# A hybrid decoder step: product-key routing over 80 sums instead of 256, 24 expert items in another stage, and FoX heads half a head later

## What is computed

```python
qry = (xi @ w_query).reshape(PEER_BLOCK, PEER_HEADS, 2, PEER_HALF)
s = jnp.einsum('thpc,pnc->thpn', qry, sub_keys)          # 2 x 128 scores per head
s1, i1 = lax.top_k(s[:, :, 0], 16)
s2, i2 = lax.top_k(s[:, :, 1], 16)
cand = (s1[..., :, None] + s2[..., None, :])             # 16 x 16 sums
cidx = (i1[..., :, None] * 128 + i2[..., None, :])
top_s, pos = lax.top_k(cand.reshape(..., 256), 16)
idx = jnp.take_along_axis(cidx, pos, axis=-1)
gate = jax.nn.softmax(top_s, axis=-1)
hid = gelu(einsum('td,thkd->thk', xi, expert_u[idx]))
y = einsum('thk,thkd->td', gate * hid, expert_v[idx])    # 8 heads x 16 experts per token
```

## Time and profile before

| | us |
|---|---|
| runs shown: median of 3 (lowest to highest) | 4675.52 (4673.76 to 4675.54) |
| profiled execution, its own time | 4657.51 |
| its span | 4655.7 |
| busy: PE, PEld, DVE | 2418.1, 1909.2, 3374.0 |
| busy: ACT, POOL | 545.6, 2361.1 |
| moved by DMA | 1513.69 MB, 325 GB/s over the span |

### The profile page before, as it was taken

The page is one execution under the profiler, slowest core; times in us unless marked ns, Lnnn a source line. Parts: engine busy times, 40 slices in busy tenths (PEclk is TensorE's granted clock), DMA queues, the critical chain, the costliest instruction groups (busy, mean ns, idle before and its releaser), DMA issues. The chain is left out here.

```text
span 4655.7 us, 35143 instructions
## 1 busy us (share of the span) xinstructions
PE 2418.1 (52%) x11713; PEld 1909.2 (41%) x11713; DVE 3374.0 (72%) x4421; ACT 545.6 (12%) x1307; POOL 2361.1 (51%) x1217
## 2 busy tenths in 40 slices
PE   6999999898488888888759564200000000000000
PEld 5888888677466656666547443100000000000000
DVE  1333333307749989989877588799898989989998
ACT  1222222200122212222210010000000000000000
POOL 1110001000226676656565322288888888888886
PEclk8999999799699999999859777655555555555555
DMA  6666666386759999999999855499999999999998
GB/s 188 210 189 203 210 203 192 112 291 228 265 209 402 410 391 393 395 391 395 339 363 408 309 203 203 154 416 422 404 419 405 411 413 420 420 412 422 411 417 355
DMA packets 443932, 1513.69 MB, mean 325 GB/s; under 512 B 42044, under 2 KB 276208, under 8 KB 277848
## 3 DMA queue, kind: packets, MB, share of 16 engines
q0 software_dynamic: 161840, 1158.85, 61.7%
q1 hardware_dynamic: 269240, 251.94, 17.0%
q10 hardware_dynamic: 12672, 100.67, 5.4%
HBM read 1384.96 MB, written 126.21 MB: 325 GB/s over the span
## 5 line engine op out<-in xcount | busy, mean ns | idle before, releaser
L1929 DVE SCALAR_TENSOR_TENSOR ex_y<-ex_ring,ex_wt,ex_y 128x2048 f32<-128x2048 f32 x538 | 1264.4, 2350 | 122.5 <-DMA ex_ring<-in_peer_v_dram,idx_all 74.4
L1914 DVE CUSTOM_DVE_ANT_0 ex_ring<-ex_ring,ex_xi 128x2048 f32<-128x2048 f32 x544 | 1244.7, 2290 | 141.2 <-DMA ex_ring<-in_peer_u_dram,idx_all 50.5
L1836 POOL DMA_INDIRECT ex_ring<-in_peer_u_dram,idx_all x384 | 794.4, 2069 | 341.2 <-DVE ex_hid L1914 136.3
L1836 POOL DMA_INDIRECT ex_ring<-in_peer_v_dram,idx_all x384 | 823.5, 2145 | 221.7 <-DVE ex_hid L1914 115.9
L1868 PE MATMUL ex_fold<-ex_y,const 128*32 128x512 f32 (+1 forms) x48 | 24.9, 683 | 1113.4 <-DVE ex_y L1929 1043.5
L1836 POOL DMA_INDIRECT ex_ring<-in_peer_v_dram,ex_idx_s x160 | 316.3, 1977 | 316.2 <-DVE ex_hid L1914 144.6
L1868 PEld LDWEIGHTS ex_fold<-ex_y,const 128*32 128x32 f32 (+1 forms) x48 | 6.3, 136 | 1131.6 <-DVE ex_y L1929 1044.4
L1836 POOL DMA_INDIRECT ex_ring<-in_peer_u_dram,ex_idx_s x160 | 315.1, 1969 | 200.3 <-DVE ex_y L1929 139.7
L843 PE MATMUL heads_b_pj<-xnT_b,lead 128*128 128x304 f32 x1376 | 410.3, 436 | 5.1 <-PEq L270 3.7
L843 PE MATMUL heads_a_pj<-xnT_a,heads_a_w 128*128 128x256 f32 x1216 | 310.1, 393 | 1.7 <-DMA heads_a_w<-in_w_in_dram 1.7
L843 PEld LDWEIGHTS heads_b_pj<-xnT_b,lead 128*128 128x128 f32 x1376 | 255.6, 198 | 79.4 <-issue 15.0
(11 more groups left out here) (568 smaller groups left out, 4156.3 us busy)
## 6 DMA issues: line engine op xcount, KB each, us to landing
lead<-w_scratch SPq DMA_DIRECT2D x43, 1024.0 KB, 9.1
heads_a_w<-in_w_in_dram SPq DMA_DIRECT2D x38, 1024.0 KB, 6.1
w_scratch<-heads_a_w ACTq DMA_DIRECT2D x38, 1024.0 KB, 4.4
lead<-in_w_in_dram SPq DMA_DIRECT2D x26, 1024.0 KB, 5.7
w_scratch<-lead ACTq DMA_DIRECT2D x26, 1024.0 KB, 4.6
heads_b_w<-w_scratch SPq DMA_DIRECT2D x21, 1024.0 KB, 9.5
out_a_w<-in_w_out_dram SPq DMA_DIRECT2D x7, 2048.0 KB, 14.3
w_out_scratch<-out_a_w ACTq DMA_DIRECT2D x7, 2048.0 KB, 9.5
```

The source lines that it names most:

```text
L1836: pool.indirect_dma_start(self.ring[:, i % RING, :], None, self.tables[which], bass.IndirectOffsetOnAxis(ap=self.index(s, g, k), axis=0)). ...
L1914: nc.vector.tensor_tensor_reduce(ring, ring, self.tokens(s)[:], 1.0, 0.0, ALU.mult, ALU.add, self.hid[:, g % 2, k:k + 1]).then_inc(self.se ...
L1929: nc.vector.scalar_tensor_tensor(y, ring, wt, y, ALU.mult, ALU.add).then_inc(self.sem["consumed"], 1)
```

## The change

Three things are changed.

1. **Routing.** With both lists sorted, a pair (i, j) of the 256 can be among the best 16 only if (i+1)(j+1) is at most 16. The 80 sums kept are first[0] with all 16 of second, first[1..7] with second[0..7], and first[8..15] with second[0]. The positions in these 80 are turned back into a pair by five small instructions on VectorE (`last`, `second`, `place`). ScalarE makes the tables of indices (three copies, once `scores_read` is there), minus the best sum (`neg`), and the exponentials with it as bias, one per tile, each with its sum; VectorE's cast of the indices, subtraction, sum over the gates and copy of the index are gone.
2. **Items.** `OVERLAP` gives heads_b 306 items instead of 330 and route_b 72 instead of 48; the total of 448 stays.
3. **Half a head later.** FoX head h begins at mark 100 h + 50. The projections have marks that are 37.5 later, and the gate of GDN (`G_Z`) is projected before FoX's three segments. Items now stand over marks 0 to 850.

```diff
-OVERLAP = {"norm": 14, "heads": 330, "out": 48, "ffn": 8, "route": 48}
+OVERLAP = {"norm": 14, "heads": 306, "out": 48, "ffn": 8, "route": 72}
...
-G_Q, G_K, G_V, F_Q, F_K, F_V, G_Z, F_OG = range(8)
+G_Q, G_K, G_V, G_Z, F_Q, F_K, F_V, F_OG = range(8)
...
 def segment_mark(j, step):
-    return 12.5 * (j - 6) + 12.5 * step / KT
+    return 12.5 * (j - 3) + 12.5 * step / KT
+
+def fox_mark(h):
+    return 100.0 * h + 50
...
             def fox():
                 for h in range(HEADS):
-                    at, n, qkv = 100.0 * h, h + 1, B.f_qkvT[:, h % 2]
+                    at, n, qkv = fox_mark(h), h + 1, B.f_qkvT[:, h % 2]
...
             def items():
                 for i in range(quota):
-                    yield 100.0 * HEADS * (i + 0.5) / quota
+                    yield (100.0 * HEADS + 50) * (i + 0.5) / quota
                     share.take(dve, i + 1)
...
-                act.wait_ge(sem["centred"], h + 1)
-                nc.scalar.activation(B.gate[:], B.gate[:], ACT.Exp).then_inc(sem["exped"], 1)
+                act.wait_ge(sem["scores_read"], h + 1)
+                if h >= 1:
+                    act.wait_ge(sem["picked"], h)
+                nc.scalar.copy(B.table[:, 0, :, 0:1], B.at[:, :, 0, 0:1])
+                nc.scalar.copy(B.table[:, 0, :, 1:], B.at[:, :, 0, :])
+                nc.scalar.copy(B.table[:, 1, :, 0:TOPK], B.at[:, :, 1, :]).then_inc(sem["tabled"], 1)
+                act.wait_ge(sem["best_found"], h + 1)
+                nc.scalar.mul(B.neg[:], B.best[:, :, 0], -1.0).then_inc(sem["negated"], 1)
+                act.wait_ge(sem["negated"], h + 1)
+                for t in range(T):
+                    last = nc.scalar.activation(B.gate[:, t, :], B.best[:, t, :], ACT.Exp, bias=B.neg[:, t:t + 1],
+                                                accum_out=B.sum[:, t:t + 1])
+                last.then_inc(sem["exped"], 1)
...
-                order.mark(nc.vector.tensor_copy(B.atf[:], B.at[:]))
-                order.link(nc.vector.tensor_tensor(B.cand[:], B.top[:, :, 0, :].unsqueeze(3).to_broadcast([P, T, TOPK, TOPK]),
-                                                   B.top[:, :, 1, :].unsqueeze(2).to_broadcast([P, T, TOPK, TOPK]), ALU.add))
-                top16(order, [(B.cand[rows[t], t].rearrange("p a b -> p (a b)"), B.best[rows[t], t, :], B.pos[rows[t], t, :])
-                              for t in range(T)])
-
-                nc.vector.tensor_tensor(B.gate[:], B.best[:], B.best[:, :, 0:1].to_broadcast([P, T, TOPK]), ALU.subtract
-                                        ).then_inc(sem["centred"], 1)
+                first, second = B.top[:, :, 0, :], B.top[:, :, 1, :]
+                order.mark(nc.vector.tensor_tensor(B.cand[:, :, 0:TOPK], first[:, :, 0:1].to_broadcast([P, T, TOPK]), second, ALU.add))
+                order.mark(nc.vector.tensor_tensor(
+                    B.cand[:, :, TOPK:72].rearrange("p t (a b) -> p t a b", b=8),
+                    first[:, :, 1:8].unsqueeze(3).to_broadcast([P, T, 7, 8]),
+                    second[:, :, 0:8].unsqueeze(2).to_broadcast([P, T, 7, 8]), ALU.add))
+                order.mark(nc.vector.tensor_tensor(B.cand[:, :, 72:CANDS], first[:, :, 8:], second[:, :, 0:1].to_broadcast([P, T, 8]),
+                                                   ALU.add))
+                order.wait()
+                if h >= 1:
+                    dve.wait_ge(sem["exped"], h)
+                top16(order, [(B.cand[rows[t], t, :], B.best[rows[t], t, :], B.pos[rows[t], t, :]) for t in range(T)])
+                dve.sem_inc(sem["best_found"], 1)
                 share.take(dve, h * PARTS + 3)
...
                 order.link(nc.vector.tensor_copy(B.posf[:], B.pos2[:]))
+                order.mark(nc.vector.scalar_tensor_tensor(B.last[:], row, 9.0, column, ALU.is_equal, ALU.mult))
+                order.mark(nc.vector.tensor_scalar(B.second[:], row, 1.0, 8.0, ALU.is_equal, ALU.mult))
+                order.wait()
+                order.mark(nc.vector.tensor_tensor(B.place[:, 0], row, B.last[:], ALU.add))
+                order.mark(nc.vector.tensor_tensor(B.place[:, 1], column, B.last[:], ALU.subtract))
+                order.wait()
+                order.link(nc.vector.tensor_tensor(B.place[:, 1], B.place[:, 1], B.second[:], ALU.add))
+                dve.wait_ge(sem["tabled"], h + 1)
...
-                order.link(nc.vector.scalar_tensor_tensor(B.pick[:, 0], B.pick[:, 0], float(KEYS), B.pick[:, 1],
-                                                          ALU.mult, ALU.add))
-                order.mark(nc.vector.tensor_copy(mem["idx_all"][:, group.own, h, :], B.pick[:, 0]))
+                dve.sem_inc(sem["picked"], 1)
+                order.mark(nc.vector.scalar_tensor_tensor(mem["idx_all"][:, group.own, h, :], B.pick[:, 0], float(KEYS),
+                                                          B.pick[:, 1], ALU.mult, ALU.add))
                 dve.wait_ge(sem["exped"], h + 1)
-                order.link(nc.vector.tensor_reduce(B.sum[:], B.gate[:], AX_X, ALU.add))
```

More of the change, by code:

```diff
@@ L47 @@
 KEYS = 128
+CANDS = 80
 SEGS = 4
@@ L2282, in _ @@
+                order.mark(nc.vector.tensor_tensor(B.cand[:, :, 72:CANDS], first[:, :, 8:], second[:, :, 0:1].to_broadcast([P, T, 8]),
[5 more added lines that the diff above has]
+                dve.sem_inc(sem["best_found"], 1)
                 share.take(dve, h * PARTS + 3)
-                order.mark(nc.vector.tensor_scalar(B.pos2[:, 0], B.pos[:], 4, None, ALU.logical_shift_right))
@@ L2285, in _ @@
-                order.mark(nc.vector.tensor_scalar(B.pos2[:, 1], B.pos[:], TOPK - 1, None, ALU.bitwise_and))
+                row, column = B.posf[:, 0], B.posf[:, 1]
+                order.mark(nc.vector.tensor_scalar(B.pos2[:, 0], B.pos[:], 3, None, ALU.logical_shift_right))
+                order.mark(nc.vector.tensor_scalar(B.pos2[:, 1], B.pos[:], 7, None, ALU.bitwise_and))
                 order.wait()
                 order.link(nc.vector.tensor_copy(B.posf[:], B.pos2[:]))
+                order.mark(nc.vector.scalar_tensor_tensor(B.last[:], row, 9.0, column, ALU.is_equal, ALU.mult))
@@ L2288, in _ @@
                 for s in range(2):
+                    n = TOPK + 1 - s
+                    hot, shape = B.hot[:, :, :, 0:n], [P, T, TOPK, n]
                     order.link(nc.vector.tensor_tensor(
[L2290 to L2291 removed]
+                        hot, B.place[:, s].unsqueeze(3).to_broadcast(shape),
+                        cst("iota", 0, n).unsqueeze(1).unsqueeze(1).to_broadcast(shape), ALU.is_equal))
@@ L2292, in _ @@
                     order.link(nc.vector.tensor_tensor(
-                        B.hot[:], B.hot[:], B.atf[:, :, s, :].unsqueeze(2).to_broadcast([P, T, TOPK, TOPK]), ALU.mult))
-                    order.link(nc.vector.tensor_reduce(B.pick[:, s], B.hot[:], AX_X, ALU.add))
-                order.link(nc.vector.scalar_tensor_tensor(B.pick[:, 0], B.pick[:, 0], float(KEYS), B.pick[:, 1],
-                                                          ALU.mult, ALU.add))
-                order.mark(nc.vector.tensor_copy(mem["idx_all"][:, group.own, h, :], B.pick[:, 0]))
+                        hot, hot, B.table[:, s, :, 0:n].unsqueeze(2).to_broadcast(shape), ALU.mult))
@@ L2298, in _ @@
+                    order.link(nc.vector.tensor_reduce(B.pick[:, s], hot, AX_X, ALU.add))
+                dve.sem_inc(sem["picked"], 1)
+                order.mark(nc.vector.scalar_tensor_tensor(mem["idx_all"][:, group.own, h, :], B.pick[:, 0], float(KEYS),
+                                                          B.pick[:, 1], ALU.mult, ALU.add))
                 dve.wait_ge(sem["exped"], h + 1)
-                order.link(nc.vector.tensor_reduce(B.sum[:], B.gate[:], AX_X, ALU.add))
                 order.link(nc.vector.reciprocal(B.rec[:], B.sum[:]))
```

27 lines of the change are left out of this document (13 added, 14 removed).

## The result

The changed kernel takes **4597.8 us** (median of 4 runs, 4593.4 to 4599.3) against 4674.6 (4 runs, 4667.3 to 4675.5): ratio 0.9837, 95% interval 0.982 to 0.9854. The prediction was 4623.5, its range 4583 to 4668. The profiled executions differ by less than the medians: 4655.7 - 4596.2 = 59.5 us of span.

A forecast was written before the change was run, and what follows sets the result against it. Bounds: TensorE in heads_a, VectorE in route_a and route_b, DMA, VectorE and TensorE together in heads_b, DMA in the last stage. Terms -6, -13, -66 and +33 sum to -52 us: 4623.5 us against the median, range 4583 to 4668.

The forecast's parts named there:

- The routing search: route_a and route_b: searching 80 columns instead of 256 saves VectorE time, -13 us and -22 us over eight heads.
- rival 5: route_a: the narrower search does nothing, as TensorE's handover holds the head at 18 us; 4636 us, chance 0.04.
- The small instructions: Routing on VectorE: five added behind the search take 0.8 us; starts are 0.09 us apart unlinked, 0.21 linked.
- the forecast's own parts: heads_b: projections 26, head 0 118, seven heads 868, last half head 43, close 13; 1068 us against 1134, -66.
- the 124 taken: heads_b: 124 us a head, DMA at 94%, down from 134.0, because DMA, VectorE and TensorE are coupled.
- rival 2: heads_b: TensorE has room, heads follow the DMA engines at 120 us, route_a at its best; 4592 us, chance 0.15.
- 121: heads_b: us a head if TensorE has room and only the DMA engines set the pace; stage 21 us shorter still.
- forecast as 0: Last stage: instructions and first moment as before, DMA share 0.99, so it only shifts and its length does not change.
- Against the median: Whole kernel: 4605.5 us from the profiled execution, moved up by the 18 us between profile and median to 4623.5.
- heads_a, -6: heads_a: TensorE's work unchanged, only idle ends can change, less of the level chain at the end; -6 us, bounds -15 and +10.
- +55 in route_b: route_b: 24 moved items at 2.40 us each add 57.6 us, less 2.4 for one falling into the starting wait.
- Rivals 3 and 4: heads_b: TensorE sets heads at 130 us, 4665 in all (0.12); or the delta-rule chain at 134, 4694 (0.07).

The follow-up runs named there:

- control: The kernel before, unchanged, run against itself: 4685.8 us, ratio 1.0001.
- experiments 2 and 5 to 10: Half-head shift alone on the kernel before (0.9851); the changed kernel with other first projections, FoX mark, item counts or item marks (0.9743 to 0.9879).
- experiment 5: The changed kernel with six projections instead of three ahead of head 0 in both groups: 4623.9 us, ratio 0.9879.
- experiments 7 to 10: The changed kernel with 330 items in heads_b, 354, 330 over marks 22 to 850, 330 over -20 to 850: 4585.1, 4601.0, 4598.1, 4564.4 us.
- experiment 3: The kernel before with only the items changed, 306 in heads_b and 72 in route_b: 4672.5 us, ratio 0.9975.
- experiment 7: The changed kernel with 330 items in heads_b and 48 in route_b, as before the change: 4585.1 us, ratio 0.9794.

## Why the prediction was right, and where it was short

**Right, and in part by luck.** The routing search: -12.9 in route_a and -21.0 in route_b alone, forecast -13 and -22; the fear that TensorE's handover holds route_a at 18 us (rival 5) did not come. The small instructions cost what the neighbouring rows said. By the Trainium skill ("VectorE: DVE Perf Modes", the TRN2 errata) each has a fixed latency. They do last 0.17 to 0.19 us for 32 columns, but start 0.11 us apart where nothing links them and 0.21 where something does. heads_b: -66.8 against -66, by the forecast's own parts: first GDN head at 143.4 us of the stage (26 + 118 = 144), seven heads 861.5 (868), then 62.5 (43 + 13 = 56). Five heads of seven ran at 119, under the 124 taken: they follow the DMA engines at 0.97, which is the rate of rival 2. The Trainium skill ("Perfetto Trace Analysis", Identifying the Most-Contended Engine) judges TensorE's room by its weight-load busy time, from which the forecast had 121; for these five heads the trace agrees. Two longer ones, with 28 us more between them, brought the mean to 123.1. So the 124 was met partly by luck: the forecast spread one loss from coupling over every head, and the runs show five heads without it and two with stalls of their own, at a gather and at the writing out of finished sums. The last stage's +11.2, forecast as 0, lies inside the 1665.6 to 1682.2 of all profiles.

**The step that failed: "Against the median".** The sum of -52 was made against the profiled execution, and the 18 us between it and the median were then added to the result. That takes for granted that the changed kernel's executions lie as far above its profile. They do not: with FoX at GDN's marks before spreads over 59 us (4659 to 4718, 29 runs), and its control, items alone and routing alone over 41, 29 and 38 (12 runs each); the kernels of experiments 2 and 5 to 10 and the changed one, with FoX 38 or 50 marks later, over 6 to 21 (4 to 6 runs each; fewer runs show less of a spread, but the standard deviation about each kernel's mean is 5.1 us in experiments 2 and 5 to 10 together, 41 runs, against 15.2 about each chip's mean in the 60 of before). Six projections first (experiment 5) leaves it small, so it goes with FoX's place, or with that of `G_Z` and the later projections, which moved in the same kernels and were not parted from it. In the one long execution profiled, two thirds of the extra time (19.2 of 28.6 us) are in heads_a, where its clock is 0.91 instead of 0.93. Over all profiles heads_a is 863.0 to 882.5 us in the five with FoX at GDN's marks and 835.3 to 842.4 in the seven whose heads_a is that of the changed kernel. 18 of the missing 26 us are this. Why the clock stays low longer in some executions is not shown.

**The term that was mis-sized: heads_a, -6.** It is -25.2 in the profile, outside the bounds of -15 and +10. The text said that TensorE's work stays the same, so only its idle ends can change, and then counted one end alone, and not the clock. The two ends of the stage, up to the end of the first GDN head and from the end of the seventh on, before and after:

```profile
54.00:215.70 161.70, 149.60 (x759) 129.22 (x760) 37.37 (x105) 27.62 (x73) 9.57 (x11) 0.91 0.74 225
825.90:917.30 91.40, 71.23 (x378) 60.45 (x377) 34.26 (x99) 23.59 (x57) 10.44 (x12) 0.77 0.21 75
```

```profile
54.00:185.70 131.70, 125.05 (x653) 108.46 (x653) 34.72 (x97) 26.18 (x60) 9.42 (x11) 0.92 0.75 223
794.20:892.20 98.00, 85.52 (x486) 73.27 (x485) 34.78 (x108) 29.74 (x73) 10.50 (x12) 0.88 0.34 119
```

At steady pace a matmul with its share of idle takes 102/569 = 0.179 us. The first end was 25.6 us over that pace and is 14.6 over: -11. The last was 23.6 over and is 10.9 over: -13. Over the whole stage TensorE's idle time falls by 13.5 us, from 863.0 - 817.6 = 45.4 to 838.2 - 806.3 = 31.9. The rest is mostly the clock: in the last end it is 0.88 instead of 0.77. Experiment 5 tries the first end alone: 14.5 of its 18 us come there. Its other 4 lie behind the seventh head, where experiments 7 to 10, with the heads_a of the changed kernel, have them too. The last end was not tried alone.

**The items.** The forecast had +55 in route_b for them; experiment 3 has +53.4, and the step from 330 to 306 behind the half head 55.9. What they give in heads_b was right in the sum. But the sum never asked whether 24 is a good number: experiment 7 puts 306 items in heads_b 11 us behind 330 once FoX stands half a head later. By these profiles the change without this part is the better one; the intervals of the two ratios, 0.982 to 0.9854 and 0.9758 to 0.983, still overlap.

**Rivals 3 and 4** (TensorE or the chain sets the head) are out: the heads are 123.1 us apart where they had 130 and 134, and experiment 3 takes items away in the old order and the heads shorten from 134.0 to 127.2.

## What to carry to other kernels

Before a forecast from one profile is set against a median, ask how far executions of that program spread and in which stage; a change can take away the spread itself. Count work that fills an in-order engine at both ends of a stage: projections spent ahead of a dependent chain are missing beside it. When a wait at a stage's start ends on a transfer or copy, put independent work into it; eight items moved there took 16 us off the stage, while 24 moved to another stage cost 11.
